# A hybrid decoder step on Trainium2: the mixer's decode values spread from block diagonal layouts, and its decode states read as the moving operand in quarters of the array

## The reference

```
cm_new = decay[..., None, None] * cm + jnp.einsum('bhs,bshv,bshd->bhvd', w_end, vc, kc)     # mLSTM, one token
num = ... + jnp.einsum('bht,bhvd,bthd->bthv', w_inter, cm, qc)
h_new = jnp.exp(acum[..., -1])[..., None, None] * h + jnp.einsum('bgrs,bsgrp,bsgn->bgrpn', w_end, xc, bc)
y = y + jnp.einsum('btgn,bgrpn,bgrt->btgrp', cc, h, jnp.exp(acum))
s_new = decay[:, None, None] * s + jnp.einsum('hs,bshd,bshv->bhdv', w_end, kc, vc)
```

## Time and profile before

| what | value |
|---|---|
| median of 3 runs | 1915.89 us (1913.73 to 1925.07) |
| profiled execution | 1909.86 us, span 1908.0 us, mean granted clock 0.972 |
| PE busy | 95% of the span |
| DVE, ACT, POOL busy | 68%, 56%, 19% |
| mixer loop, layer 0 | first spread at 202.90 us, first output product at 316.37 us |
| mixer loop, layer 1 | first spread at 905.29 us, first output product at 1019.28 us |

### The profile page before, as it was taken

One profiled execution on the slowest core, in us unless ns is written; L12 is line 12 of the kernel. 1 busy time (PEld: TensorE's weight loads), 2 busy tenths in 40 slices (PEclk: granted clock), 3 DMA queues, 4 the chain that ended last, 5 costly groups with the idle time before them and its releaser, 6 DMA issues.

```text
span 1908.0 us, 30795 instructions
## 1 busy us (share of the span) xinstructions
PE 1808.2 (95%) x12287; PEld 1648.4 (86%) x12287; DVE 1290.4 (68%) x1836; ACT 1060.4 (56%) x1709; POOL 367.7 (19%) x334
## 2 busy tenths in 40 slices
PE   7999989999899998999999999799899999989997
PEld 6999979997799998999989987688788888878886
DVE  4764776542556567655855533698879978978986
ACT  4445445443545454445445534377667866766775
POOL 4970332000000007932231000040012003000000
PEclk9999989999899998999979999899999999999999
DMA  7554345547655453553446367379959978986994
GB/s 296 177 172 163 122 141 182 200 170 288 226 175 193 168 207 126 191 180 134 144 124 248 134 248 292 121 267 355 358 212 350 370 259 298 363 330 228 355 363 167
DMA packets 73603, 434.07 MB, mean 227 GB/s; under 512 B 8373, under 2 KB 13045, under 8 KB 33013
## 3 DMA queue, kind: packets, MB, share of 16 engines
q1 hardware_dynamic: 71332, 425.19, 61.8%
q0 software_dynamic: 2128, 6.92, 1.0%
HBM read 407.59 MB, written 24.48 MB: 226 GB/s over the span
## 4 chain that ended last, share of the span: by engine, by line
PE 81%; DVE 10%; DMA 5%; ACT 2%; issue 1%; SPq 0%; DVEq 0%; ACTq 0%
PE ps L1134 16%; PE ps L576 14%; PE ps L577 14%; PE ps L578 13%; PE ps L1160 8%; DVE wL L301 3%; DMA ring<-x_down_dram 2%; PE ps L1117 2%; PE ps L556 2%; DVE stream L1886 2%; PE ps L816 1%; DMA ring<-x_gu_dram 1%; PE ps L1172 1%; DVE proj L1943 1%; PE ps L797 1%; ACT wH L295 1%
## 5 line engine op out<-in xcount | busy, mean ns | idle before, releaser
L301 DVE TENSOR_TENSOR wL<-ring,wH 128x1024 fp32r<-128x1024 f32 (+1 forms) x704 | 834.4, 1216 | 383.6 <-ACT wH L295 379.2
L295 ACT ACTIVATE wH<-ring 128x1024 fp32r<-128x1024 f32 (+1 forms) x704 | 709.1, 1026 | 280.2 <-PE ps L578 117.6
L576 PE MATMUL ps<-hH,wH 128*128 128x264 f32 x1376 | 400.7, 291 | 14.3 <-DVE hL L1669 7.8
L577 PE MATMUL ps<-hL,wH 128*128 128x264 f32 x1376 | 392.5, 285 | 0.0
L578 PE MATMUL ps<-hH,wL 128*128 128x264 f32 x1376 | 392.0, 285 | 0.0
L1134 PE MATMUL ps<-wH,projR 128*128 128x512 f32 (+1 forms) x1152 | 294.0, 377 | 0.3 <-ACT wH L295 0.3
L576 PEld LDWEIGHTS ps<-hH,wH 128*128 128x128 f32 x1376 | 261.1, 190 | 23.0 <-issue 19.0
L577 PEld LDWEIGHTS ps<-hL,wH 128*128 128x128 f32 x1376 | 261.7, 190 | 0.6
L578 PEld LDWEIGHTS ps<-hH,wL 128*128 128x128 f32 x1376 | 260.5, 189 | 0.0
L576 PE MATMUL ps<-projR,wH 128*128 128x264 f32 (+1 forms) x816 | 239.0, 293 | 15.8 <-DVE projR L2041 7.1
L1134 PEld LDWEIGHTS ps<-wH,projR 128*128 128x128 f32 x1152 | 211.0, 188 | 35.9 <-issue 1.4
(11 more groups left out here) (365 smaller groups left out, 2394.6 us busy)
## 6 DMA issues: line engine op xcount, KB each, us to landing
ring<-x_gu_dram SPq DMA_DIRECT2D x96, 1024.0 KB, 7.1
ring<-x_down_dram SPq DMA_DIRECT2D x60, 1024.0 KB, 7.0
ring<-w_in_dram SPq DMA_DIRECT2D x56, 1024.0 KB, 4.9
ring<-x_gu_dram SPq DMA_DIRECT2D x48, 768.0 KB, 5.7
ring<-w_gu_dram SPq DMA_DIRECT2D x22, 1024.0 KB, 4.9
stream<-states_dram SPq DMA_DIRECT2D x32, 512.0 KB, 4.2
ring<-w_out_dram SPq DMA_DIRECT2D x16, 1024.0 KB, 4.9
o_states_dram<-stream SPq DMA_DIRECT2D x32, 512.0 KB, 4.4
```

The lines of the kernel that those rows point to most:

```text
L295: act.activation(wH[:, buf * PIECE:buf * PIECE + n], slot(s, half * n, n), ACT.Copy).then_inc(hi_ready, 1)
L301: dve.tensor_tensor(wL[:, buf * PIECE:buf * PIECE + n], slot(s, half * n, n), f32(wH[:, buf * PIECE:buf * PIECE + n]), ALU.subtract).then_ ...
L576: pe.matmul(dst, wh, high(k0 + k), start=k0 + k == 0, stop=False)
L577: pe.matmul(dst, wh, low(k0 + k), start=False, stop=False)
```

## The change

The values of a group are laid out once as a block diagonal matrix by `value_blocks` on DVE: each row of `vrow` is repeated eight times along the free dimension and multiplied with a 0/1 mask (`R_SAMPLE`), so that row (unit, sample b) is nonzero in block b alone. `spread` then needs one selector per unit (`R_UNIT`) and two products of 512 columns. The layouts lie in `tmp` (mLSTM), and for the other two groups in the place of the input projection's last piece in `wH` and `wL`.

`read_out` turns the operands round: q_b, broadcast to 32 columns, is stationary, and the state is the moving operand, 128 columns. Four samples write to four quarters of the partitions (32 rows each, all equal), and two such sets lie beside one another, in bank 0 for u below 12 and in bank 6 for the rest. The result is now a row, so ACT copies the 128x256 patch to SBUF (`copy_rows`), PE transposes it in two pieces (`turn_rows`), and `read_in` takes every 32nd column. Since bank 0 is also the spread's first half, `read_out(u)` waits until `update(u+1)` has used its first half, and `spread` waits for an earlier `read_in`. The waits for `dec_y` ahead of L699 and of the SSD blocks are replaced by waits for `ml_state` and `ssd_h`. `const_round` is folded into `row_high`, and counts of `dec_mv` and `v_low` are doubled.

```diff
+        vdiag = [view("vdiag0", NB * P, F32R, tmp_at)]
...
-            return 7 if u < NH else 6
+            return 0 if u < NH + SP else 6
+        rows_in = tmp[:, 1664:1920]
+        def read_rows(u, c_, r_):
+            return bank(read_bank(u), c_ * P, P, 32, 32 * r_)
...
@@ ml_d(h)
                     if h:
-                        pe.wait_ge(dec_y, l * UNITS + h)
+                        turn_rows(h - 1)
+                        pe.wait_ge(ml_state, n)
...
@@ ssd_d(j)
+                    turn_rows(i - 1)
                     if j:
-                        pe.wait_ge(dec_y, l * UNITS + i)
+                        pe.wait_ge(ssd_h, n)
...
@@ ret_d(h), between the blocks and the state products
+                    turn_rows(NH + SP + h - 1)
...
@@ spread(u)
-                        for b in range(NB // 2):
-                            part, at = divmod((u - first) * NB + hf * (NB // 2) + b, 32)
-                            ins = pe.matmul(bank(hf, b * P, P), row_of(part, at), vrow[g][:, :], start=True, stop=True)
-                        ins.then_inc(dec_bc, 1)
+                        if hf == 0 and 0 <= u - 2 < NH + SP:
+                            pe.wait_ge(dec_y, l * UNITS + u - 1)
+                        one = constR[:, R_UNIT + u - first:R_UNIT + u - first + 1].to_broadcast([P, P])
+                        pe.matmul(bank(hf), one, values_of(l, g)[:, hf * 512:(hf + 1) * 512], start=True, stop=True).then_inc(dec_bc, 1)
...
@@ read_out(u)
-                    pe.wait_ge(dec_S, 2 * (n + 1))
-                    if u:
+                    if u < NH + SP:
+                        pe.wait_ge(dec_S, 2 * (n + 1) + 1)
+                    else:
+                        pe.wait_ge(dec_S, 2 * (n + 1))
+                        pe.wait_ge(ssd_h, (l + 1) * SP)
                         pe.wait_ge(dec_y, n)
-                    if u < NH:
-                        pe.wait_ge(ml_state, l * NH + u + 1)
-                    elif u < NH + SP:
-                        pe.wait_ge(ssd_h, l * SP + u - NH + 1)
-                    for b in range(NB):
-                        ins = pe.matmul(bank(read_bank(u), 448 + b, 1), state(u)[:, b * P:(b + 1) * P], q[:, b:b + 1], start=True, stop=True)
+                    for c_ in range(2):
+                        for r_ in range(4):
+                            b = 4 * c_ + r_
+                            ins = pe.matmul(read_rows(u, c_, r_), q[:, b:b + 1].to_broadcast([P, 32]), state(u)[:, b * P:(b + 1) * P], start=True, stop=True)
+                    ins.then_inc(dec_mv, 1)
+                def turn_rows(u):
+                    pe.wait_ge(dec_row, l * UNITS + u + 1)
+                    for c_ in range(2):
+                        ins = pe.transpose(bank(read_bank(u), c_ * P, P), rows_in[:, c_ * P:(c_ + 1) * P], ident)
                     ins.then_inc(dec_mv, 1)
...
@@ end of the mixer on PE
                 post_sum(POSTS - 2)
+                turn_rows(UNITS - 1)
...
@@ ACT
+                def copy_rows(u):
+                    n = l * UNITS + u
+                    act.wait_ge(dec_mv, 2 * n + 1)
+                    if u:
+                        act.wait_ge(dec_y, n)
+                    act.activation(rows_in, bank(read_bank(u), 0, 2 * P), ACT.Copy).then_inc(dec_row, 1)
...
                         weights_of(i + 1)
+                    if i:
+                        copy_rows(i - 1)
...
+                copy_rows(UNITS - 1)
                 post_square(POSTS - 2)
...
@@ DVE: after projection tile 44 for g = 0, in iteration 1 for g = 1, in iteration 7 for g = 2
+                def value_blocks(g):
+                    if g == 1:
+                        dve.wait_ge(piece_done, Q0 + N_PROJ)
+                    dve.wait_ge(v_low, 2 * (3 * l + g) + 1)
+                    dve.tensor_tensor(values_of(l, g)..., f32(vrow[g][:, :])..., f32(constR[:, R_SAMPLE:R_SAMPLE + NB])..., ALU.mult).then_inc(v_low, 1)
...
@@ read_in(u)
-                    dve.wait_ge(dec_mv, l * UNITS + u + 1)
-                    ys = bank(read_bank(u), 448, NB)
+                    dve.wait_ge(dec_mv, 2 * (l * UNITS + u) + 2)
+                    ys = bank(read_bank(u), 0, 2 * P).rearrange("p (c r w) -> p c r w", c=2, r=4)[:, :, :, 0]
```

More of the change, by code:

```diff
@@ L66 @@
 R_ID, R_MASK, R_SEL, N_ROUND = 0, 128, 256, 320
+R_UNIT, R_SAMPLE = R_SEL + 16, R_SEL + 48
 UNITS = NH + SP + RH
@@ L226, in program @@
         row_high, row_low = sem("row_high"), sem("row_low")
-        const_round = sem("const_round")
         v_zero, v_in, v_rows, v_high, v_low = (sem(n) for n in ("v_zero", "v_in", "v_rows", "v_high", "v_low"))
-        dec_decay, dec_bc, dec_S, dec_mv, dec_y = (sem(n) for n in ("dec_decay", "dec_bc", "dec_S", "dec_mv", "dec_y"))
+        dec_decay, dec_bc, dec_S, dec_mv, dec_row, dec_y = (sem(n) for n in ("dec_decay", "dec_bc", "dec_S", "dec_mv", "dec_row", "dec_y"))
         pst_out = [sem(f"pst_out{k}") for k in range(3)]
@@ L250, in program, with values_of @@
         y_out = sem("y_out")
+        def values_of(l, g):
+            if g == 0:
+                return vdiag[0]
+            at = (LAYER_PIECE[l] + N_PROJ - 1) % BUFS * PIECE
+            return (wH, wL)[g - 1][:, at:at + NB * P]
         def bank(b, lo=0, n=512, rows=P, r0=0):
@@ L489, in _ @@
                         sp.wait_ge(state_out[u % STATE_SLOTS], 16 * state_count(l, u))
-                        sp.wait_ge(dec_mv, l * UNITS + u + 1)
+                        sp.wait_ge(dec_mv, 2 * (l * UNITS + u) + 1)
                         load_state(l, u + STATE_SLOTS)
@@ L501, in _ @@
                     load(t["w_out"][l, j])
-                sp.wait_ge(dec_mv, (l + 1) * UNITS)
+                sp.wait_ge(dec_mv, 2 * (l + 1) * UNITS - 1)
                 for u in range(UNITS - STATE_SLOTS, UNITS):
@@ L676, in ml_a @@
                         pe.wait_ge(gate_bc_in, l + 1)
-                        pe.wait_ge(const_round, 1)
+                        pe.wait_ge(row_high, 1)
                         pe.wait_ge(row_low, l + 1)
@@ L690, in ml_d @@
                         pe.wait_ge(nden_done, l + 1)
-                        pe.wait_ge(v_low, 3 * l + 2)
+                        pe.wait_ge(v_low, 2 * (3 * l + 1) + 1)
                     else:
@@ L789, in spread @@
                     if u == first:
-                        pe.wait_ge(v_low, 3 * l + g + 1)
+                        pe.wait_ge(v_low, 2 * (3 * l + g) + 2)
                     for hf in range(2):
@@ L824, in post_sum @@
                     else:
-                        pe.wait_ge(dec_y, l * UNITS + NH)
                         pe.wait_ge(ml_state, (l + 1) * NH)
@@ L829, in post_sum @@
                     elif p == 2:
-                        pe.wait_ge(v_low, 3 * (l + 1))
+                        pe.wait_ge(v_low, 2 * (3 * l + 2) + 1)
                     tiles = post_group(p)[1]
@@ L1260, in _ @@
                         act.activation(rows[:, :], const[:, 0:SEQ], ACT.Copy, scale=0.0)
-                    act.activation(constR[:, :], conv[:, 0:N_ROUND], ACT.Copy).then_inc(const_round, 1)
+                    act.activation(constR[:, :], conv[:, 0:N_ROUND], ACT.Copy).then_inc(row_high, 1)
                 for j in range(N_PROJ):
@@ L1833, in _ @@
                     elif j == 18:
-                        dve.wait_ge(row_high, l + 1)
+                        dve.wait_ge(row_high, l + 2)
                         dve.tensor_tensor(rowA[32:44, :], cum_a, f32(rowA[0:12, :]), ALU.subtract)
@@ L1844, in _ @@
                         value_low(0, 2, 0, NH * NB)
+                    elif j == 44:
+                        dve.wait_ge(row_high, 1)
+                        value_blocks(0)
                     elif j == 53:
@@ L1890, in read_in, with eight @@
                 def read_in(u):
-                    dve.wait_ge(dec_mv, l * UNITS + u + 1)
-                    ys = bank(read_bank(u), 448, NB)
+                    dve.wait_ge(dec_mv, 2 * (l * UNITS + u) + 2)
+                    ys = bank(read_bank(u), 0, 2 * P).rearrange("p (c r w) -> p c r w", c=2, r=4)[:, :, :, 0]
+                    def eight(x):
+                        return x.rearrange("p (c r) -> p c r", c=2)
                     if u < NH:
-                        ins = dve.tensor_tensor(tile(proj, Q_ML + u, SEQ, NB), ys, rden[:, u * NB:(u + 1) * NB], ALU.mult)
+                        ins = dve.tensor_tensor(eight(tile(proj, Q_ML + u, SEQ, NB)), ys, eight(rden[:, u * NB:(u + 1) * NB]), ALU.mult)
                     elif u < NH + SP:
                         j = u - NH
-                        st(dve.scalar_tensor_tensor(out=yT, in0=tile(conv, j, SEQ, NB), scalar=pcol(l, D_SKIP + j), in1=ys, op0=ALU.mult, op1=ALU.add))
+                        st(dve.scalar_tensor_tensor(out=eight(yT), in0=eight(tile(conv, j, SEQ, NB)), scalar=pcol(l, D_SKIP + j), in1=ys, op0=ALU.mult, op1=ALU.add))
                         ins = dve.tensor_tensor(tile(proj, Z + j, SEQ, NB), tile(proj, Z + j, SEQ, NB), yT, ALU.mult)
                     else:
```

(12 more changed lines are left out.)

4 lines of the change are left out of this document (3 added, 1 removed).

## The result

The changed kernel takes 1920.84 us (median of 20 runs, 1914.38 to 1931.09), the kernel before 1914.99 beside it (20 runs, 1904.02 to 1925.07): a ratio of 1.0036, 95% interval 1.0019 to 1.0054. It is slower by 5.9 us between the medians and by 6.9 by the ratio, on the side that was forecast and inside the range, but by less than half of the 14 us forecast. The profiled execution took 1919.62 us (span 1917.8).

A forecast was written before the change was run, and what follows sets the result against it. DVE's chain was to bound mLSTM units, PE's own chain retention units. 4.4 + 0 + 0.6 + 2 = 7 us a layer, 14 in all, gave 1924, as a median 1930 us; forecast range 1918 to 1942, wider 1905 to 1954.

The forecast's parts named there:

- clock term: All stages: one or two mLSTM units at 1.2 GHz, partly offset in SSD; +2 us a layer (-5 to +13).
- mLSTM, +4.4 a layer: mLSTM units: read-out waits for half of the next update, delaying `outputs`; 0.74 us slower, six times a layer.
- SSD, 0 a layer: SSD units: turn waits for ACT's copy, 0.45 us later; shorter spread returns 0.38; 0 a layer (-4 to +4).
- the balance is about even: SSD units at 1.2 GHz: turn and spread double, so the later turn and shorter spread about cancel.
- some of it back from the SSD stage: SSD stage: part of the mLSTM clock loss returns because the one-column read-outs go; within +2 us a layer.
- rival 1: SSD stage stays at 2.4 GHz, 6.6 us a layer come back; 1908 us (1900 to 1920), chance 0.25.
- Rival 1's 7.5: SSD block groups start 9.71 us apart; without half-rate excess of blocks (1.32) and spread (0.85), 7.5 us.
- Retention, +0.6 a layer: Retention units: PE's work falls 1.09 us a unit, but turn waits for ACT's copy; +0.6 a layer (-2 to +2).
- the end, +0.3: End of the retention stage: two copies and turns in line, 1.2 us, less one shorter read-out, 0.9; +0.3.
- Prices: New instructions: read-out 0.75 us (0.59 to 1.01), turn 0.22, copy 0.37; all three `value_blocks` cost nothing.
- rival 3: Read-out's quarters don't overlap: mLSTM +6.1 us a layer, retention +1; 1944 us, chance 0.08.
- Rival 2: Clock falls in most mLSTM units: 5 x 2.7 us a layer in place of 2; 1953 us, chance 0.17.

The follow-up runs named there:

- own bank: Changed kernel with the mLSTM read-out's rows in bank 7 in place of bank 0, waits adapted; 1911.82 us, ratio 0.9991.
- filled kernels: Kernel before and changed kernel, each with ten unread transposes in five of six SSD units; 1902.20 us (ratio 0.9936) and 1914.14 us (1.0004).
- late order: Changed kernel with read-out and row copy moved earlier in retention units alone, last turn ahead of the last sum but one; 1912.10 us, ratio 1.0000.
- spread alone: Kernel before with the change's `spread` and `value_blocks` only, `read_out` and `read_in` as before; 1906.20 us, ratio 0.9944.
- filled kernel before: Kernel before with ten unread transposes on PE in each SSD unit but the first; 1902.20 us, ratio 0.9936.

## Why the prediction failed, and what of it held

The step that failed is the clock term, +2 us a layer for all three stages. Measured it is between -0.7 and -2.8 in layer 0, since the SSD stage won back more by its clock than the other two stages lost. With that in its place, the other terms as forecast (4.4 + 0 + 0.6) give 2.2 to 4.3 a layer, around the 2.9 and 3.5 that were measured. The mechanism was in the prediction; size and sign of the term were wrong.

- **mLSTM, +4.4 a layer: the mechanism right, the size in part by luck.** Read-out 0.57 (taken 0.75), blocks 1.44 (232.72 - 231.28; 1.32), turn 0.22, state products 0.65 (0.75), start of the read-out 1.17 (1.15): the unit is 0.56 longer, not 0.74. From the first `update` to the seventh that is 3.9 us in layer 0, 1.5 of it the half-rate unit; the first blocks of the SSD stage come another 1.8 later. Together 5.7, or 4.2 without the half-rate unit, against 4.4: six units of 0.74 were forecast, and about 0.56 each in the units and more at the way into the SSD stage came. The own bank shows the cause: without the wait a unit is back at 6.54. DVE's wait is 1.27 us (1.5 forecast), most of it ahead of the read-in and not for the state products.
- **SSD, 0 a layer, and the clock, +2 a layer: the terms that failed.** That "the balance is about even" is what the middle units of both filled kernels show (7.5 us a unit); over the stage up to 2 us of saved work may be there. But the stage took 5.6 us less, as the granted clock rose from 0.77 and 0.70 to 0.87. The clock term foresaw "some of it back from the SSD stage" and still set +2 a layer for all stages. Measured in layer 0 it is about +1.5 in the mLSTM (8.58 for 7.10), -3.5 to -5.6 in the SSD and about +1.3 in the retention stage (2.84 for 1.50): -0.7 to -2.8 together, inside its bounds of -5 to +13 and 2.7 to 4.8 from the value taken. The forecast was off by 3.75 a layer (14 for two layers, 6.5 measured), so this term is most of the miss or more than all of it; the retention stage goes the other way. This is rival 1's mechanism by half; the changed kernel idles about 2 us before the turn, and the stage did not reach 1.00. Rival 1's 7.5 is right in part by luck: it took 1.32 us for the half-rate excess of the SSD blocks, which is 0.88 (1.96 for 1.08), and left out 1.1 us of sums and row products at half rate.
- **Retention, +0.6 a layer: mis-sized, +2.8, beyond its bound of +2.** The place was right: the turn waits for the copy in every unit but the last. Without the half-rate products behind the first unit's gap it is +1.5, inside the bound. The part that was mis-sized is the end, +0.3 in the forecast and 2.0 measured (5.79 for 3.81), where PE waits for ScalarE at the next to last turn (0.92 us) and at the sum ahead of the last turn (1.34). The Trainium skill, "TensorEngine Tiling (Array Packing)", PSUM Bottleneck, warned of the copy. This trace agrees that the turn waits for the copy, but the late order shows that the place of the hand-over did more than the copy's 0.37 us: with the same copy 2.3 of the 2.8 us come back.
- **Prices.** Quarters overlap, so rival 3 falls. 0.57 is next to 0.59, the end where half the columns halve the record, and far from 1.01. The first and third `value_blocks` cost nothing that shows; the second lies under DVE's wait in the changed kernel, and costs 1.1 us a layer once that wait is gone, as in the spread alone and with the own bank.
- **Rival 2** (most mLSTM units slow) did not come: one unit of six, in layer 1 also the way into the SSD stage.

In sum +5.7, -5.6 and +2.8 make 2.9 in layer 0, 3.5 in layer 1, against 7 each.

Left open: which gap lowers the clock. After 2.08 us of idle PE the blocks at 279.05 ran at full rate, and those behind 2.14 us at 300.11 were at half rate by 301.85. It is shown that filling the SSD gaps raises the clock of that stage, not why one gap costs and the next does not. The filled kernel before even lost 2.1 and 2.9 us of its gain in other stages of layer 1, where nothing was changed (0.95 and 0.89).

## What to carry to other kernels

A read-out that no longer fills the engine pays only if its hand-over is taken out of the chain as well: the same change cost 6 to 7 us with it behind a shared bank and at the end of ScalarE's round, and gave 36 with both put right, part of it as clock. Where a stage's granted clock is under 1.00, price it at both levels and ask what the change does to TensorE's gaps, before comparing work. A term with several microseconds of clock in its bounds should not be set near zero because it can go both ways.

## What the runs showed of the hardware

- Useless work made a kernel faster: ten transposes (1.25 us) in each of ten units raised the SSD stage's clock from 0.77 and 0.70 to 1.00 and 0.97, and took 7.0 and 7.7 us off it, and 10 us off the whole (1912.63 to 1902.20).
- Sixteen fp32 records of 32 stationary and 128 moving columns take 0.57 us over four quarters of the array, 1.87 in one.
